# A two-layer hybrid trunk on eight cores: a new program with a phase conv, multiplied attention weights and 1024 tokens a pass

## What is computed

```python
u = rms_norm(h, norm_mix_g)
b_a, c_a, h_a, v_b, g_b = split(u @ w_in)            # 5 x 512
y_a = b_a * causal_dwconv(c_a * h_a, conv_a_w)       # 3 taps
cb  = causal_dwconv(v_b * sigmoid(g_b), conv_b_w) + conv_b_bias   # 31 taps
y_b = silu(layer_norm(cb))
h = h + concat(y_a, y_b) @ w_out
q = rms_norm(h, norm_x_g) @ w_q                      # 4 heads of 256
k, v = split(rms_norm(mem, norm_mem_g) @ w_kv)
h = h + (softmax(q k^T / 16) v) @ w_xo
h = h + relu(rms_norm(h, norm_ffn_g) @ w_up)**2 @ w_down          # 4096 wide
```

## Time and profile before

| | us |
|---|---|
| runs, median of 3 | 3916.6 (3911.92, 3916.6, 4286.07) |
| profiled execution, span of the slowest core (2) | 3919.6 |
| span of the fastest core | 3905.3 |
| PE busy | 3703.1 |
| DVE busy | 1753.3 |
| ACT busy | 1255.7 |
| POOL busy | 33.1 |

### The profile page before, as it was taken

How to read it: one execution, slowest core, us unless ns; L and a number is a source line. 1 busy time by engine, 2 the same in 40 slices (tenths; PEclk the granted TensorE clock), 3 DMA queues, 4 the chain that set the end, 5 groups by cost and what they waited for, 6 DMA issues and landing times.

```text
span 3919.6 us, 47835 instructions; the slowest of 8 cores (3905.3 to 3919.6 us)
## 1 busy us (share of the span) xinstructions
PE 3703.1 (94%) x16968; PEld 1657.2 (42%) x16968; DVE 1753.3 (45%) x2756; ACT 1255.7 (32%) x2123; POOL 33.1 (1%) x66
## 2 busy tenths in 40 slices
PE   4688798999999999999999999999999999999998
PEld 2233343444444444444444444444444444444443
DVE  3352542535535264543525454353644525454452
ACT  2142151423414233241424325242241523233141
POOL 0000000000000000000000000000000000000000
PEclk8899999999999999999999999999999999999999
DMA  9999999444353434534345343444435343343432
GB/s 190 227 219 225 226 217 258 170 151 149 129 196 127 151 130 150 193 129 151 129 149 184 140 150 123 168 160 151 141 132 201 126 145 137 143 171 135 156 122 94
DMA packets 99702, 631.44 MB, mean 161 GB/s; under 512 B 9360, under 2 KB 10640, under 8 KB 27024
## 3 DMA queue, kind: packets, MB, share of 16 engines
q1 hardware_dynamic: 90544, 563.37, 40.3%
q0 software_dynamic: 8928, 65.02, 11.0%
HBM read 611.57 MB, written 81.79 MB: 177 GB/s over the span
## 4 chain that ended last, share of the span: by engine, by line
PE 76%; DMA 13%; DVE 6%; issue 3%; ACT 2%; another core or an unknown queue 1%; DVEq 0%; POOL 0%; ACTq 0%; SPq 0%; POOLq 0%
PE ps L306 42%; PE ps L388 20%; PE ps L400 12%; DMA wbf<-arena 10%; DVE arena L321 3%; PE ps L311 3%; DMA arena<-wts 3%; DVE arena L331 2%; ACT arena L316 2%; DVE arena L326 0%; DMA arena<-wbf 0%; DMA arena<-memT 0%; DVEq L159 0%; ACT arena L317 0%
## 5 line engine op out<-in xcount | busy, mean ns | idle before, releaser
L306 PE MATMUL ps<-arena 128*128 128x512 bf16 (+1 forms) x9744 | 2168.2, 381 | 131.7 <-ACT arena L316 38.1
L306 PEld LDWEIGHTS ps<-arena 128*128 128x128 bf16 x9744 | 957.1, 99 | 1294.6 <-issue 180.7
L316 ACT ACTIVATE arena<-arena 128x512 bf16<-128x512 f32 (+2 forms) x963 | 579.7, 655 | 1477.7 <-DVE arena L321 1446.9
L388 PE MATMUL ps<-arena 128*128 128x512 bf16 x4096 | 901.4, 379 | 5.7 <-DMA arena<-wts 5.7
L321 DVE TENSOR_TENSOR arena<-arena 128x512 bf16<-128x512 f32 (+1 forms) x848 | 565.2, 689 | 413.4 <-ACT arena L316 394.7
L316 ACT ACTIVATE arena<-ps 128x512 f32<-128x512 f32 (+1 forms) x832 | 473.6, 598 | 817.1 <-PE ps L306 616.3
L321 DVE TENSOR_TENSOR arena<-arena,ps 128x512 f32<-128x512 f32 x384 | 252.4, 685 | 1025.8 <-PE ps L388 771.9
L400 PE MATMUL ps<-arena 128*128 128x512 bf16 x2560 | 578.8, 380 | 58.6 <-DVE arena L321 50.6
L388 PEld LDWEIGHTS ps<-arena 128*128 128x128 bf16 x4096 | 400.8, 98 | 491.3 <-issue 10.1
L331 DVE SCALAR_TENSOR_TENSOR arena<-arena 128x512 bf16<-128x512 f32 (+3 forms) x656 | 462.3, 742 | 193.4 <-ACT arena L316 159.3
L400 PEld LDWEIGHTS ps<-arena 128*128 128x128 bf16 x2560 | 246.2, 98 | 376.1 <-issue 90.6
(11 more groups left out here) (13 smaller groups left out, 110.1 us busy)
## 6 DMA issues: line engine op xcount, KB each, us to landing
arena<-wbf SPq DMA_DIRECT2D x442, 1024.0 KB, 4.9
wbf<-arena SPq DMA_DIRECT2D x62, 1024.0 KB, 18.8
arena<-wts POOLq DMA_DIRECT2D x62, 1024.0 KB, 23.4
arena<-xT SPq DMA_DIRECT2D x8, 2048.0 KB, 17.3
outT<-arena SPq DMA_DIRECT2D x8, 2048.0 KB, 7.7
arena<-memT SPq DMA_DIRECT2D x1, 1024.0 KB, 8.0
arena<-vecs SPq DMA_DIRECT2D x1, 184.5 KB, 2.5
arena<-ident SPq DMA_DIRECT2D x1, 64.0 KB, 1.7
```

Of the source, the lines that this page charges most:

```text
L306: ins = e.matmul(ps.ap, lhsT=l, rhs=r, start=(i == 0), stop=(i == n - 1))
L316: return e.activation(out=out.ap, in_=in_.ap, func=func, scale=scale)
L388: ins = e.matmul(ps.ap, lhsT=w3[:, k, :], rhs=src.full[:, k * T:(k + 1) * T], start=(k == 0), stop=(k == nk - 1))
```

## The change

All of the program is new; the mathematics is the same.

- *Tokens.* A pass over the weights takes TT = 1024 tokens, as two streams s = 0, 1 of 512, interleaved group by group; 4 passes. The host permutes x so that within 512 tokens the order is (phase q = t mod 4, t div 4).
- *Weights.* Pieces of 128x2048 (0.5 MB as bf16) in a ring of ten slots. All pieces of w_in, w_out, w_up, w_down are read as f32 with a cast on every pass (POOL's queue). Only the conv weights and the two products below are kept as bf16 and loaded on SP.
- *31-tap conv.* Four phases of 32 channels fill 128 partitions, and a banded 128x128 weight does four taps in four phases: nine matmuls of 256 columns for each of 16 channel groups. The input is laid out by 32 small SBUF-to-SBUF DMAs a layer and pass on SP, and the output back by 32 more.
- *Attention.* Once, for each layer, K·W_q^T and V·W_xo are multiplied (`setup`); scores are then xg times the first, with tokens on the partitions: maximum, exp with sum, reciprocal and scaling per 128 tokens and two heads; 64 matmuls with an identity transpose the probabilities back; one projection with the second product follows.
- *Norms.* Squares are added on DVE (`Rms.add`), one matmul with ones per 512 tokens closes the sum, run a few groups later (`later`). The factors of a norm are applied after the matmul: RA (1/rms), RB (1/rms squared), RC for the down projection's output.
- *Gates.* `v * sigmoid(g)` and the gated conv have multiplies on POOL. `bg` holds work that `tick` releases one item a group: the layer norm of the conv (inside the second half of the gated conv), conv weight builds, final norm, staging of the next x.
- A write on DVE, ACT or POOL now also waits for the engine's own earlier uses of the same granule.

Cut to what the text speaks of:

```diff
-T = 512
+T = 512
+NS = 2
+TT = NS * T
+PH = 4
+TAU = T // PH
+CW = NS * TAU
+NM = 9
+NG = 16
+RING = 10
+SLOT = 2 * NM * 128
...
+        def ring_pump():
+            while ring["loaded"] < min(len(seq), ring["freed"] + RING):
+                i = ring["loaded"]
+                kind, cid = seq[i]
+                slot = slots[i % RING]
+                if kind == "f":
+                    S.op("pool", lambda e, o=slot.full[:, 0:2048], s=wts[cid]: e.dma_start(out=o, in_=s),
+                         writes=[slot.r(0, 2048)], dma_sem=sem[f"wc{i % RING}"])
+                else:
+                    if cid not in wb_ready:
+                        return
+                    n = SLOT if cid % NWB_L < W_AQ else 2048
+                    S.op("sp", lambda e, o=slot.full[:, 0:n], s=wbf[cid][:, 0:n]: e.dma_start(out=o, in_=s),
+                ring["loaded"] += 1
...
+            def add(self, src):
+                self.n += 1
+                if self.n == 1:
+                    act(self.acc.r(), src, AF.Square)
+                    return
+                sq = rot("sq", sqs)
+                act(sq.r(), src, AF.Square)
+                tt("dve", (self.acc if self.n < 8 else self.accb).r(), self.acc.r(), sq.r(), ALU.add)
...
+        def resid_tail(s, m, gnext, rms):
+            hm = h[s].c(m)
+            rms.add(hm)
+            if gnext is not None:
+                act(xg.c(m, s * T, (s + 1) * T), hm, AF.Copy, scale=vcol(gnext + m), extra_reads=[vref])
...
+                        m = ci * 4 + j
+                        ps = pss[j] if ci == 0 else grp(sl[j // 2], j % 2, src, s)
+                        tt("dve", h[s].c(m), h[s].c(m), ps, ALU.add)
+                        resid_tail(s, m, gnext, rm[s])
+                    if ci == 1:
+                        out[s] = later(4, lambda s=s: fin(s, rm[s]))
...
+        def conv_build(l, i):
+            stage = cstage[i % 2]
+            st3 = stage.full.rearrange("p (k q) -> p k q", q=32)
+            S.op("dve", lambda e: e.tensor_tensor(out=st3, in0=e3, in1=w3_, op=ALU.mult),
+                 reads=[cstf.r(), tapb.r()], writes=[stage.r()])
+            wb_store(l * NWB_L + W_CONV + i, stage.r())
...
+                        psg = grp(sg, jj, xg, s)
+                        lz[s].run()
+                        t = tmp()
+                        tt("dve", t.r(), psg, RA[s].r(), ALU.mult)
+                        act(t.r(), t.r(), AF.Sigmoid)
+                        tt("pool", t.r(), t.r(), RA[s].r(), ALU.mult)
+                        psv = grp(sv, jj, xg, s)
+                        tt("dve", glu.c(j, s * T, (s + 1) * T), psv, t.r(), ALU.mult)
...
+            for a in range(4):
+                items = []
+                for q in range(PH):
+                    src = glu.full[a * 32:(a + 1) * 32, :].rearrange("p (j s q t) -> p j s q t", j=4, s=NS, q=PH)[:, :, :, q, :]
+                    for s in range(NS):
+                        o = glc.full[q * 32:(q + 1) * 32, 4 * a * glc.stride:(4 * a + 4) * glc.stride]
+                        o = o.rearrange("p (g t) -> p g t", t=glc.stride)[:, :, HM + s * TAU:HM + (s + 1) * TAU]
...
+                S.dma_group("sp", items, sem[f"si{a}"])
...
+                        psc = grp(sc, jj, xg, s)
+                        t = tmp()
+                        tt("dve", t.r(), psc, RB[s].r(), ALU.mult)
+                        psh = grp(sh, jj, xg, s)
+                        c = rot("chb", chb)
+                        cv = cva[s * 2 + jj]
+                        tt("dve", c.r(2 * TAU, 2 * TAU + T), psh, t.r(), ALU.mult)
+                        copy("pool", c.r3(0, 2, 1, TAU), c.r3(4, 6, 0, TAU - 1))
+                        hh = chh[l].r(2 * j, 2 * j + 2)
+                        h3 = Ref(hh.ap.unsqueeze(2), "sb", hh.lo, hh.hi)
+                        copy("pool", c.r3(0, 2, 0, 1), h3)
+                        copy("pool", h3, c.r3(4, 6, TAU - 1, TAU))
+                        act(cv.r(), c.r(2 * TAU, 2 * TAU + T), AF.Copy, scale=vcol(wa + 2 * 4 + j), extra_reads=[vref])
+                        stt("dve", cv.r(), c.r(TAU, TAU + T), vcol(wa + 4 + j), cv.r(), ALU.mult, ALU.add, extra_reads=[vref])
+                        stt("dve", cv.r(), c.r(0, T), vcol(wa + j), cv.r(), ALU.mult, ALU.add, extra_reads=[vref])
+                        tt("pool", cv.r(), cv.r(), RA[s].r(), ALU.mult)
+                for s in range(NS):
+                    for jj in range(2):
+                        j = 2 * jp + jj
+                        psb = grp(sb_, jj, xg, s)
+                        tt("dve", ycat.c(j, s * T, (s + 1) * T), psb, cva[s * 2 + jj].r(), ALU.mult)
...
+            for cc in range(8):
+                slot = ring_get(b_id(l, W_CONV + cc))
+                ps = next_ps()
+                for gg in range(2):
+                    g = 2 * cc + gg
+                    g0 = g * glc.stride
+                    mm(sub(ps, gg * CW, (gg + 1) * CW),
+                       [(slot.full[:, (gg * NM + m) * 128:(gg * NM + m + 1) * 128], glc.full[:, g0 + HM - m:g0 + HM - m + CW]) for m in range(NM)],
+                       [slot.r(), glc.c(g)])
+                tick()
+                ring_free(1)
+                for gg in range(2):
+                    g = 2 * cc + gg
+                    act(cb.c(g), sub(ps, gg * CW, (gg + 1) * CW), AF.Identity, bias=vcol(vb + V_CBB + g), extra_reads=[vref])
+                pair = cb.r(2 * cc * CW, (2 * cc + 2) * CW)
+                sq = ln_q if cc == 0 else tmp()
+                act(sq.r(), pair, AF.Square)
...
+                if cc > 0:
+                    tt("dve", (ln_qb if cc == 7 else ln_q).r(), ln_q.r(), sq.r(), ALU.add)
...
+                ts("dve", ln_m.r(), sub(ps, 0, CW), 1.0 / 512, None, ALU.mult)
+                tt("dve", ln_v.r(), ln_m.r(), ln_m.r(), ALU.mult)
+                stt("dve", ln_v.r(), sub(ps, CW, 2 * CW), 1.0 / 512, ln_v.r(), ALU.mult, ALU.subtract)
+                ts("dve", ln_v.r(), ln_v.r(), 0.0, None, ALU.max)
+                act(ln_v.r(), ln_v.r(), AF.Ln, scale=1.0, bias=eps_ref.ap, extra_reads=[eps_ref])
+                act(ln_v.r(), ln_v.r(), AF.Exp, scale=-0.5)
+                touch(AF.Silu)
...
+                tt("dve", blk, blk, bc(ln_m), ALU.subtract)
+                tt("dve", blk, blk, bc(ln_v), ALU.mult)
+                for g in range(4 * a, 4 * a + 4):
+                    act(yb.c(g), cb.c(g), AF.Silu, scale=vcol(vb + V_LNG + g), bias=vcol(vb + V_LNB + g), extra_reads=[vref])
...
+            bg.append(ln_stats)
+            for a in range(4):
+                bg.append(lambda a=a: ln_apply(a))
+            chb_part(1)
+            drain_bg()
+            bgwork()
...
+                for tb in range(4):
+                    ps = next_ps()
+                    t0 = s * T + tb * 128
+                    mm(ps, [(xg.full[:, k * TT + t0:k * TT + t0 + 128], wk(sl[k // 4], 512)[:, k % 4, :]) for k in range(8)],
+                       [sl[0].r(0, 2048), sl[1].r(0, 2048)] + [xg.c(k, s * T, (s + 1) * T) for k in range(8)])
+                    tick()
+                    lz[s].run()
+                    S.op("dve", lambda e, o=mx.ap, i_=p3.ap: e.tensor_reduce(out=o, in_=i_, axis=AX.X, op=ALU.max),
+                         reads=[p3], writes=[mx])
+                    ts("dve", nb, mx, rs, -1.0, ALU.mult, ALU.mult, extra_reads=[rtok.r()])
+                    t = tmp()
+                    for hh in range(2):
+                        act(t.r(hh * NMEM, (hh + 1) * NMEM), sub(ps, hh * NMEM, (hh + 1) * NMEM), AF.Exp, scale=rs,
+                            bias=nb.ap[:, hh:hh + 1], extra_reads=[rtok.r(), nb], accum=smalls[i].r(4 + hh, 5 + hh))
+                    S.op("dve", lambda e, o=ri.ap, i_=sm.ap: e.reciprocal(out=o, in_=i_), reads=[sm], writes=[ri])
+                    for hh in range(2):
+                        ts("dve", P.c(tb, hh * NMEM, (hh + 1) * NMEM), t.r(hh * NMEM, (hh + 1) * NMEM), ri.ap[:, hh:hh + 1], None,
+                           ALU.mult, extra_reads=[ri])
...
+            sl0 = [ring_get(keys[0]), ring_get(keys[1])]
+            scores(0, 0, sl0)
+            scores(0, 1, sl0)
+            ring_free(2)
+            sl1 = [ring_get(keys[2]), ring_get(keys[3])]
+            scores(1, 0, sl1)
+            trans(0, 0)
+            trans(0, 1)
+            scores(1, 1, sl1)
+            ring_free(2)
+            trans(1, 0)
+            return lambda: trans(1, 1)
...
+        def ffn_up(l):
+            for cc in range(8):
+                sl = [ring_get(w_id(l, C_UP + 2 * cc)), ring_get(w_id(l, C_UP + 2 * cc + 1))]
+                for s in range(NS):
+                    for j in range(4):
+                        ps = grp(sl[j // 2], j % 2, xg, s)
+                        t = tmp()
+                        act(t.r(), ps, AF.Relu)
+                        tt("dve", hid.c(cc * 4 + j, s * T, (s + 1) * T), t.r(), t.r(), ALU.mult)
+                ring_free(2)
...
+                    t = tmp()
```

(3 more changed lines are left out.)

1183 lines of the change are left out of this document (625 added, 558 removed).

## The result

The changed kernel takes 1.0835 times the time of the kernel before (95% interval 1.0809 to 1.0861): 4245.1 and 4235.4 us against 3916.6 and 3911.9. It is slower by 8.35%. The forecast was 3955 us with a range up to 4160, so the time lies outside the range, 290 us above the forecast.

A forecast was written before the change was run, and what follows sets the result against it. The old kernel was taken as PE-bound after a DMA-bound start. Matmuls 3163, one-time products 55, chain waits 514, GLU 24, start 100, setup 60, joints 20 and tail 20 sum to 3956; forecast 3955 us, range 3740 to 4160.

The forecast's parts named there:

- the clock term: Between conv and up projection, three groups of four start at lowered clock after PE idles: 1.7 us each, 5.1 a block.
- 32 take 12 us and have 20.8 us of gated conv over them: Small transfers laying out the conv's input, at 0.39 us an issue on SP, were taken as hidden behind gated conv.
- the softmax step: Attention, per 128 tokens and two heads: DVE's chain with ACT takes 3.15 us where PE needs 1.73.
- the joint: Change to the next 1024 tokens: final scaling sits in DVE's waits, 7 us at each of three, 20 in all.
- the walk: Step-by-step timing of engine queues from the last conv matmul to the up projection: loss 64.3 us a block, 514 in all.
- the loss of 100: Start, before the first DVE product: x loads, conv-weight builds and memory norm cost 100 us (60 to 130).
- the setup term: One-time products wait for 16 weight pieces each, and h loads only after their stores: 60 us (20 to 90).
- Cast loads too slow: Rival, chance 0.07: at 8 us a weight piece, up and down projections wait 35 us a block, giving 4235.
- POOL as the slow link: Rival, chance 0.14: POOL multiplies of 2.0 us in GLU and gated conv cost 10 us a block, giving 4035.
- Clock at half: Rival, chance 0.10: half clock through the waiting stretch makes four groups of four slower, 22 us a block, giving 4135.
- Short chains: Rival, chance 0.33 shared with a far cheaper start: faster softmax and residual chains, a block loses 43 us, time 3785.
- The signs I named: Forecast wrong if up/down wait for DMA, conv-to-up stretch leaves 155 to 195 us, or its clock is under 0.9.

The follow-up runs named there:

- e2: Changed kernel with each softmax step's reciprocal and scaling emitted after the next step's maximum and negated product on DVE: 4060.7 us, ratio 1.0346 to the kernel before.
- e3: Changed kernel with each residual group's square added to the running sum after the next group's add into h: 4133.2 us, ratio 1.053 to the kernel before.
- e6: e5 plus e2's order and, in W_out and xo only, e3's order: 3853.9 us, ratio 0.984 to the kernel before.
- e1: Changed kernel with the conv input's row stride raised from 264 to 320 elements, so transfer groups share no granule: 4223.4 us, ratio 1.076 to the kernel before.
- e5: e1 plus POOL's conv-history copy moved ahead of its next weight loads, holding them until the small transfers land: 4153.5 us, ratio 1.0607 to the kernel before.
- e10: e6 with memory norm behind the first mixer, layer 0's conv weights built in background, and e9's edit: 3799.6 and 3793.8 us, ratio 0.967 to the kernel before.
- e9: Changed kernel with the next h loaded after the next mixer's conv has been issued: 4221.0 us, ratio 1.075 to the kernel before.
- e7: Changed kernel with four unread 512-column matmuls added per softmax step in PE's idle time: 4237.8 us, ratio 1.082 to the kernel before.

## Why the prediction was wrong

- **What was forecast and held.** The new program does fewer matmuls and gives the gain back in chains between DVE and ACT: this mechanism is right, and e2, e3 and e6 show it by removal. Sizes: the residual period 2.17 (forecast 2.13); W_out's start to DVE's end 42.8 (40.9); the first DVE product at 87.4, inside 80 to 100; up and down without waits; the clock term, where the fours behind a wait of 4.7 us or more took 9.22, 8.39 and 8.52 us and the one behind 1.54 took 7.07, so about 5 a block, as counted; GLU at 3.5 a pair (3.5) and POOL's multiply at 1.27 (1.3).
- **The step that failed.** "32 take 12 us and have 20.8 us of gated conv over them", at 0.39 us an issue. Three things were off. An issue takes 0.64 to 0.68, not 0.39; that row was of the store of h, another kind of transfer. SP waits between the groups of eight, 32 issues taking 37.6 us instead of 12. And the landing was priced at nothing, while beside cast loads it comes up to 16 us late. The fallback "a block would lose up to 12" was no upper bound: it priced SP's issues alone. Measured, the conv takes 35 to 39 us instead of 15.6, which is 22 of the 27 us that the stretches without a joint are over. Four more follow behind it, since W_out starts 41 us after the conv and not 37. e1 took SP's waits away (29 us in all) and e5 the landing (60), by holding back the cast loads.
- **A term too small: the softmax step**, 3.42 instead of 3.15. The two sum outputs were taken as 0.2 together; each is an instruction of its own of 0.19, and the exponential takes 0.56 from PSUM, where 0.45 was assumed from 256 elements of SBUF. Sixteen steps make 4.3 of the 9.3 us that W_out to xo is over. Residual groups make 2; some 3 are not traced further.
- **A term too small: the joint.** 7 us each were counted, for DVE alone. In the changed kernel joint stretches are 15 longer than the others. With the conv's waits gone it is 35 (e5), and e10 shows that 20 of them are the load of h ahead of the conv's weights. It costs in two ways, as e6's rows show: SP waits 8.5 us for the store, and then 2 MB land together with the piece that PE needs. e9's edit takes both away at once, so no run says how the 20 divide. I had counted DMAs by their bytes over the whole span, and neither what waits behind a waiting load nor what lands at the same moment.
- **The start and the first block.** The first W_out came at 271.5 where the walk has 272, and that is luck. The conv took 40.1 us there too instead of 15.6. It began at 141.9 where the walk has 151, and from its end to W_out it was 89.6 where the walk has 105, so the loss of 100 and the setup term were some 25 too high together. In e5, without the conv's waits, the first W_out comes at 248.9. Behind it the first block is 23 and 13 us over; 15.5 of the 23 are one wait of PE for ACT.
- **Rivals.** "Cast loads too slow" named 4235 us, which is nearly the time, but for another reason: PE waits 24 us in all for these weights, none in up or down, and a piece takes 3.1 us of the queue (29.2% of 4243 by 400) where 3.5 was taken. The cast loads cost their 20 us a block through what they delay. "POOL as the slow link" did not decide: its multiply is 1.27, and 2.11 (2.72 three times in the start) only where DVE works on two SBUF operands. "Clock at half" did not either: the clock is 0.75 to 0.91 through most of the stretch, lower than I allowed, but e7 shows that PE's speed does not set the pace of the softmax. "Short chains" is what e2 and e3 make by hand.
- **The signs I named.** Three of them spoke: the clock (0.85 on the mean from the conv to the up projection, where under 0.9 was a sign), PE's idle time of 827 where 650 to 700 was given, and PE's busy time of 3416 where 3250 was. The 166 us of busy time lie in the same stretches: PE is busy 125.7 us from the conv to the up projection (1782 to 1966) where the walk has 109.0, and 19.9 in the conv (1746 to 1782) where it has 15.6, 21 a block. In the softmax part of it e7 shows that such time is beside the path; for the rest that is not shown. From the conv to the up projection it is about 184 us (41 + 104 + 39), inside 155 to 195, and no wait for DMA fell in up or down. I had placed my tests where I expected waits, and the one that mattered lay in the conv itself.
- **The range** left out that several neighbouring terms could be short together. Transfers taken as hidden and the joints had been given no end above their value that was worth more than 12 and 7 us.

## What to carry to other kernels

When instructions of two engines hand work to and fro, work out the period of the chain in program order before counting busy shares. Emitting the end of a softmax step behind the beginning of the next took 192 us from this kernel (e2) and no instruction. A small transfer on the path is priced by its landing beside whatever bulk loads another queue may start at that moment, and a load that waits for a store is priced by what stands behind it on its queue and by what lands beside it. Remove waits in pairs where one stands behind the other: e9's edit was worth 9 us a joint before the conv's wait was gone, and 20 after.

## What the runs showed of the hardware

- A transfer of 32 KB over 32 partitions takes SP 0.64 to 0.68 us to issue (32 in 21.6), and the same size outward 0.75 (32 in 24.0), where the store of h, 2 MB over 128 partitions, takes 0.39. Its median landing is 1.9 us. Issued beside seven cast loads of 0.5 MB, the last of 32 lands 16 us after SP has issued it (e1); with those loads held back, 1.5 (e5).
- A sum output of ACT is a separate instruction of 191 ns, 256 times in the span.
- POOL's multiply of 512 elements takes 1.27 us with DVE idle or on a PSUM operand, and 2.11 beside two of DVE's passes over 1024 elements in SBUF. Such a pair of passes takes 3.43 us beside a multiply (at 1797.47) and 2.54 without one (at 1801.42): the second pass is 0.9 longer, as the multiply is. Their mean over the span, 1439 ns, mixes the two; undisturbed ones take 1.22, as in the earlier trace rows.
- The granted clock is 0.76 over 32 us of softmax in which no wait of PE is longer than 3.1 us. In the kernel before, the matmuls after a single idle time of 2.34 us ran at full speed. 0.76 is a mean between the two levels, 1.2 and 2.4 GHz. The Trainium skill, "TensorE: Matmul & The Clock Gate", section "A second HAM failure mode: psum-queue depth-cycling", says that an engine which idles briefly and often between groups swings between the levels; this row agrees. What would restore the clock inside such a stretch is left open: twice the busy time (e7) gave 0.06.
